# Two-block network on one core: head norms and the GLA gate multiplied on VectorE, with a new table of shifts

## The reference

```python
def rms_norm(x, g):
    y = x * rsqrt(mean(x * x, axis=-1) + EPS)
    return y * g

def gla_output(o, gate, norm_g, w_o):              # o: tokens x 4 heads x 128
    o = rms_norm(o, norm_g).reshape(b_, t_, GLA_V)
    return (o * silu(gate)) @ w_o

def attn_heads(q, k, v, qn_g, kn_g, tabs):         # q: 8 heads of 64, k: 2 heads of 64
    q, k = rms_norm(q, qn_g), rms_norm(k, kn_g)
    if tabs is not None:                           # latent tokens only
        q, k = rope_2d(q, tabs), rope_2d(k, tabs)
    return q, k, v
```

## Time and profile before

| | |
|---|---|
| median of three runs | 1309.15 us (1308.46 to 1309.38) |
| the profiled execution | 1308.85 us |
| its span, first to last instruction | 1306.9 us |
| mean granted clock of TensorE | 0.976 |
| VectorE busy | 896.9 us, 1636 instructions |
| ScalarE busy | 587.8 us, 978 instructions |
| GpSimd busy | 295.4 us, 235 instructions |

### The profile page before, as it was taken

The page is one execution under the profiler, slowest core; times in us unless marked ns, Lnnn a source line. Parts: engine busy times, 40 slices in busy tenths (PEclk is TensorE's granted clock), DMA queues, the critical chain, the costliest instruction groups (busy, mean ns, idle before and its releaser), DMA issues. The chain is left out here.

```text
span 1306.9 us, 19578 instructions
## 1 busy us (share of the span) xinstructions
PE 1226.5 (94%) x7720; PEld 1003.4 (77%) x7720; DVE 896.9 (69%) x1636; ACT 587.8 (45%) x978; POOL 295.4 (23%) x235
## 2 busy tenths in 40 slices
PE   6899997989998999995999999999999989799998
PEld 5767876768877778774777778888898768579997
DVE  4598766786787443798999464435776687866655
ACT  3445542445555544222433444324563554337543
POOL 0210103210115313347000030311451241201223
PEclk9999997989999999998999999999999998989999
DMA  7575476454533411121222212333653233214453
GB/s 247 202 286 189 162 268 208 164 198 146 203 129 116 142 53 61 50 65 64 81 66 65 65 65 81 97 97 105 207 175 104 82 108 97 65 36 144 156 182 113
DMA packets 49132, 168.10 MB, mean 129 GB/s; under 512 B 5841, under 2 KB 7057, under 8 KB 48785
## 3 DMA queue, kind: packets, MB, share of 16 engines
q1 hardware_dynamic: 49041, 166.86, 38.3%
HBM read 165.79 MB, written 1.05 MB: 128 GB/s over the span
## 5 line engine op out<-in xcount | busy, mean ns | idle before, releaser
L2385 DVE TENSOR_TENSOR w_lo<-w_raw,w_hi 128x1024 fp32r<-128x1024 f32 (+3 forms) x264 | 322.1, 1223 | 187.2 <-ACT w_hi L1965 186.0
L1965 ACT ACTIVATE w_hi<-w_raw 128x1024 fp32r<-128x1024 f32 (+3 forms) x264 | 270.1, 1026 | 377.0 <-issue 118.7
L1581 PE MATMUL bank<-w_hi,x_hi 128*128 128x512 f32 (+4 forms) x736 | 297.8, 405 | 16.8 <-DVE w_lo L2385 14.4
L1583 PE MATMUL bank<-w_hi,x_lo 128*128 128x512 f32 (+4 forms) x736 | 280.8, 382 | 0.0
L1582 PE MATMUL bank<-w_lo,x_hi 128*128 128x512 f32 (+4 forms) x736 | 280.4, 381 | 0.0
L1599 PE MATMUL bank<-x_hi,w_hi 128*128 128x512 f32 (+1 forms) x640 | 224.8, 351 | 1.5 <-DVE w_lo L2385 1.5
L1601 PE MATMUL bank<-x_lo,w_hi 128*128 128x512 f32 (+1 forms) x640 | 216.4, 338 | 0.0
L1600 PE MATMUL bank<-x_hi,w_lo 128*128 128x512 f32 (+1 forms) x640 | 216.3, 338 | 0.0
L1581 PEld LDWEIGHTS bank<-w_hi,x_hi 128*128 128x128 f32 x736 | 141.4, 192 | 50.1 <-DVE w_lo L2385 18.2
L1583 PEld LDWEIGHTS bank<-w_hi,x_lo 128*128 128x128 f32 x736 | 140.4, 191 | 26.9
L1582 PEld LDWEIGHTS bank<-w_lo,x_hi 128*128 128x128 f32 x736 | 141.4, 192 | 22.6
(11 more groups left out here) (359 smaller groups left out, 1801.5 us busy)
## 6 DMA issues: line engine op xcount, KB each, us to landing
w_raw<-in_w SPq DMA_DIRECT2D x172, 512.0 KB, 3.6
w_raw<-in_wm SPq DMA_DIRECT2D x48, 512.0 KB, 5.0
w_raw<-in_wo SPq DMA_DIRECT2D x40, 512.0 KB, 4.3
w_raw<-in_wy_gla SPq DMA_DIRECT2D x8, 512.0 KB, 3.5
w_raw<-in_wy_att SPq DMA_DIRECT2D x8, 512.0 KB, 3.5
w_raw<-in_wy_conv SPq DMA_DIRECT2D x8, 512.0 KB, 3.5
w_raw<-in_w SPq DMA_DIRECT2D x8, 460.0 KB, 5.0
w_raw<-in_w SPq DMA_DIRECT2D x12, 288.0 KB, 2.8
```

What stands on the lines that cost most here:

```text
L1581: mm(out, xh[:, q, col], hi[:, kk, 0:w], start=kp == 0 and kk == 0 and not with_bias, stop=False)
L1583: ins = mm(out, xl[:, q, col], hi[:, kk, 0:w], start=False, stop=last and kk == KP - 1)
L1965: do(hi, raw, ACT.Copy).then_inc(sem["cut_hi"], 1)
L2385: v.tensor_tensor(lo, raw, hi.bitcast(F32), ALU.subtract).then_inc(sem["cut_lo"], 1)
```

## The change

In a head norm GpSimd's hr_iv keeps only the power. VectorE's hr_n multiplies each head by its root and by the norm weight in one instruction of 64 columns, 8 for a query tile and 2 for a key tile. In the GLA output gla_n is gone, and gated moves to VectorE: four instructions of 128 columns multiply each head by its root and by the gate. gla_iv on GpSimd keeps its power and its product with the norm weight. The first step of the next layer that overwrites the sums (gla_ms) now waits for gated where it waited for gla_n. The product of attention and gate (y2_gate) stays on GpSimd and has a semaphore of its own. HASTE is replaced and some lengths too, so that the planner orders all engines anew, in the first block as well.

```diff
-            yield [("gla_sq", l, t), ("gla_ms", l, t), ("gla_iv", l, t), ("gla_n", l, t)]
+            yield [("gla_sq", l, t), ("gla_ms", l, t), ("gla_iv", l, t)]
...
-    "att_t_act fox": 0.3, "bias1": -0.4, "conv_ve": 1.5, "flip mix": 3, "gla_ki": -0.4, "gla_m": 6, "ln_dve": 3,
-    "loads_consts": 1.5, "lr_t": 3, "mi_x": 0.3, "mod_col": 0.8, "out_gate": 0.3, "project_y y2": 0.3}
+    "att_t_act fox": 0.3, "bias1": -0.4, "conv_g": -0.4, "conv_n": -1, "conv_silu": -0.4, "conv_ve": 1.5, "ev_ag": -0.4,
+    "ev_gate": -1, "ev_y y0": 0.3, "flip mix": 3, "flip_hi mix": 3, "fox_cols": 1.5, "gla_ki": -0.4, "gla_m": 6, "gla_tot": 6,
+    "heads_act dq": -3, "heads_dve iq": -1, "hr_add q": 1.5, "hr_iv k": 3, "hr_sq q": -0.4, "ln_dve": 3, "ln_stat": 6,
+    "loads_consts": 1.5, "lr_t": 3, "mi_act": 3, "mi_pow": 0.3, "mi_x": -0.4, "out_gate": 0.3, "project_y y2": 0.3,
+    "sub_sum": -0.4, "y2_lo": 6}
...
-    "gate_silu": 0.45, "gated": 1.95, "gla_a": 0.86, "gla_con": 0.6, "gla_cp": 1.85, "gla_cum": 0.85, "gla_dec": 0.2,
+    "gate_silu": 0.45, "gated": 1.0, "gla_a": 0.86, "gla_con": 0.6, "gla_cp": 1.85, "gla_cum": 0.85, "gla_dec": 0.14,
...
-    "gla_one": 0.54, "gla_qf": 0.43, "gla_qi": 0.6, "gla_qt": 0.48, "gla_sq": 1.25, "gla_st": 0.55, "gla_tot": 0.9,
-    "gla_z": 0.85, "gla_zero": 2.2, "heads": 0.43, "heads_act": 0.48, "heads_dve": 0.6, "hr_add": 1.25, "hr_iv": 2.3,
-    "hr_ms": 0.6, "hr_n": 1.4, "hr_sq": 1.25, "index_iw": 0.1, "index_relu": 0.45, "index_sel": 0.2, "index_top": 0.6,
+    "gla_qf": 0.3, "gla_qi": 0.89, "gla_qt": 0.48, "gla_sq": 1.25, "gla_st": 0.55, "gla_tot": 0.9, "gla_z": 1.0,
+    "gla_zero": 2.2, "heads": 0.43, "heads_act": 0.48, "heads_dve": 0.6, "hr_add": 0.96, "hr_iv": 1.58, "hr_ms": 0.6,
+    "hr_n": 1.8, "hr_sq": 1.25, "index_iw": 0.1, "index_relu": 0.45, "index_sel": 0.14, "index_top": 0.6, "index_w": 0.5,
...
-    "gated": lambda l, c, t: [("ev_gate", l, c, t), ("gla_n", l, t)],
+    "gated": lambda l, c, t: [("ev_gate", l, c, t), ("gla_iv", l, t)],
...
-    def gla_n(l, t):
-        ov = b.gv[:, t, :].rearrange("p (h n) -> p h n", h=4)
+    def gated(l, c, t):
+        dve.wait_ge("ev_gate", l, c, t)
         dve.wait_ge("gla_iv", l, t)
-        v.tensor_tensor(ov, ov, b.gms[:, t, 0:4].unsqueeze(2).to_broadcast([P, 4, P]), ALU.mult).then_inc(sem["gla_n"], 1)
+        for h in range(4):
+            part, gate = b.gv[:, t, h * P:(h + 1) * P], k.gate_home(l, t)[:, h * P:(h + 1) * P]
+            ins = v.scalar_tensor_tensor(part, part, b.gms[:, t, h:h + 1], gate, ALU.mult, ALU.mult)
+        ins.then_inc(sem["gated"], 1)
...
-        ins = v.tensor_tensor(view, view, stat[:, 2, 0:n_heads].unsqueeze(2).to_broadcast([P, n_heads, HD]), ALU.mult)
+        dve.wait_ge("consts2_in", CONSTS2)
+        for h in range(n_heads):
+            ins = v.scalar_tensor_tensor(view[:, h, :], view[:, h, :], stat[:, 2, h:h + 1], b.rows[:, l, first:first + HD], ALU.mult, ALU.mult)
...
-    def gated(l, c, t):
-        pool.wait_ge("ev_gate", l, c, t)
-        pool.wait_ge("gla_n", l, t)
-        g.tensor_tensor(b.gv[:, t, :], b.gv[:, t, :], k.gate_home(l, t), ALU.mult).then_inc(sem["gated"], 1)
...
-        g.tensor_tensor(stat[:, 2, 0:n_heads], stat[:, 1, 0:n_heads], m.half[:, 0:n_heads], ALU.pow)
-        pool.wait_ge("consts2_in", CONSTS2)
-        pool.wait_ge("hr_sq", l, what, t)
-        g.tensor_tensor(view, view, spread(gain, [P, n_heads, HD]), ALU.mult).then_inc(sem["hr_iv"], 1)
+        g.tensor_tensor(stat[:, 2, 0:n_heads], stat[:, 1, 0:n_heads], m.half[:, 0:n_heads], ALU.pow).then_inc(sem["hr_iv"], 1)
```

More of the change, by code:

```diff
@@ L759 @@
[L759 to L762, removed]
@@ new lines @@
+    "hr_n": 1.8, "hr_sq": 1.25, "index_iw": 0.1, "index_relu": 0.45, "index_sel": 0.14, "index_top": 0.6, "index_w": 0.5,
+    "lam": 0.4, "lam_dots": 0.74, "lam_exp": 0.2, "ln_dve": 1.3, "ln_pool": 3.24, "ln_pow": 0.32, "ln_stat": 0.17, "ln_x": 0.52,
+    "load": 2.0, "lr_flip": 0.43, "lr_t": 0.48, "m_hi": 0.55, "m_lo": 0.6, "mean_w": 0.2, "mi_act": 0.98, "mi_add": 1.0,
+    "mi_dve": 0.6, "mi_flip": 0.43, "mi_hi": 0.55, "mi_lo": 0.78, "mi_ms": 0.1, "mi_pow": 0.71, "mi_sq": 1.1, "mi_x": 1.04,
@@ L959 @@
     "gla_sq": lambda l, t: [("gla_o1", l, t), ("gla_o2", l, t)],
-    "gla_ms": lambda l, t: [("gla_sq", l, t), ("gla_n", l - 1, t)],
+    "gla_ms": lambda l, t: [("gla_sq", l, t), ("gated", l - 1, GG, t)],
     "gla_iv": lambda l, t: [("gla_ms", l, t)],
-    "gla_n": lambda l, t: [("gla_iv", l, t)],
     "hr_sq": lambda l, what, t: [*BLOCK1_OVER, ("ev2", l, KKV if what == "k" else AQ, t)],
@@ L1032 @@
           "ln_dve": "ln_steps", "conv_ve": "conv_steps", "conv_rs": "conv_steps", "conv_dev": "conv_steps",
-          "conv_n": "conv_steps", "ev_ag": "ev_gate", "y2_gate": "gated", "y2_hi": "flip_hi", "y2_lo": "flip_lo"}
+          "conv_n": "conv_steps", "ev_ag": "ev_gate", "y2_hi": "flip_hi", "y2_lo": "flip_lo"}
 def signal_of(stage):
@@ L2828, in gla_ms @@
         if l > 0:
-            dve.wait_ge("gla_n", l - 1, t)
+            dve.wait_ge("gated", l - 1, GG, t)
         one = dve.own(v.tensor_reduce(b.gms[:, t, 0:4], b.gtmp[:, g, :].rearrange("p (h n) -> p h n", h=4), AXX, ALU.add))
@@ L2854, in hr_n @@
     def hr_n(l, what, t):
-        src, n_heads, stat = head_view(what, t)
+        src, n_heads, stat, first = head_view(what, t)
         view = src.rearrange("p (h d) -> p h d", d=HD)
         dve.wait_ge("hr_iv", l, what, t)
-        ins = v.tensor_tensor(view, view, stat[:, 2, 0:n_heads].unsqueeze(2).to_broadcast([P, n_heads, HD]), ALU.mult)
+        dve.wait_ge("consts2_in", CONSTS2)
+        for h in range(n_heads):
+            ins = v.scalar_tensor_tensor(view[:, h, :], view[:, h, :], stat[:, 2, h:h + 1], b.rows[:, l, first:first + HD], ALU.mult, ALU.mult)
         if t in X_TILES:
@@ L2955, in vector_engine @@
              "gla_one": gla_one, "gla_la": gla_la, "gla_qi": gla_qi, "gla_kt": gla_kt, "gla_m": gla_m, "gla_st": gla_st,
-             "gla_o2": gla_o2, "gla_ms": gla_ms, "gla_n": gla_n, "hr_ms": hr_ms, "hr_n": hr_n, "ak_t": ak_t,
+             "gla_o2": gla_o2, "gla_ms": gla_ms, "gated": gated, "hr_ms": hr_ms, "hr_n": hr_n, "ak_t": ak_t,
              "aq_dve": aq_dve, "a_max": a_max, "a_inv": a_inv, "a_t_dve": a_t_dve, "att_out2": att_out2,
@@ L3109, in gla_iv, with head_view @@
         g.tensor_tensor(ov, ov, spread(b.rows[:, l, 0:P], [P, 4, P]), ALU.mult).then_inc(sem["gla_iv"], 1)
-    def head_view(what, t, l):
+    def head_view(what, t):
         if what == "k":
-            return b.kkv[:, t, QK2:QK2 + P], AKV, b.ams[:, 0, t], b.rows[:, l, P + HD:P + 2 * HD]
-        return b.aq[:, t, :], AH, b.ams[:, 1, t], b.rows[:, l, P:P + HD]
+            return b.kkv[:, t, QK2:QK2 + P], AKV, b.ams[:, 0, t]
+        return b.aq[:, t, :], AH, b.ams[:, 1, t]
     def hr_sq(l, what, t):
-        src, n_heads, stat, gain = head_view(what, t, l)
+        src, n_heads, stat = head_view(what, t)
         i, before = slot("gtmp", "hr_sq", l, what, t)
@@ L3125, in hr_iv @@
     def hr_iv(l, what, t):
-        src, n_heads, stat, gain = head_view(what, t, l)
-        view = src.rearrange("p (h d) -> p h d", d=HD)
+        _, n_heads, stat = head_view(what, t)
         pool.wait_ge("hr_ms", l, what, t)
-        g.tensor_tensor(stat[:, 2, 0:n_heads], stat[:, 1, 0:n_heads], m.half[:, 0:n_heads], ALU.pow)
-        pool.wait_ge("consts2_in", CONSTS2)
-        pool.wait_ge("hr_sq", l, what, t)
-        g.tensor_tensor(view, view, spread(gain, [P, n_heads, HD]), ALU.mult).then_inc(sem["hr_iv"], 1)
+        g.tensor_tensor(stat[:, 2, 0:n_heads], stat[:, 1, 0:n_heads], m.half[:, 0:n_heads], ALU.pow).then_inc(sem["hr_iv"], 1)
     def hr_add(l, what, t):
-        src, n_heads, stat, gain = head_view(what, t, l)
+        src, n_heads, stat = head_view(what, t)
         i, j = slot("gtmp", "hr_sq", l, what, t)[0], slot("gtmp", "hr_n", l, what, t)[0]
```

33 lines of the change are left out of this document (17 added, 16 removed).

## The result

| | before | after |
|---|---|---|
| median of 4 runs each, same chip | 1308.81 us (1308.32 to 1309.38) | 1287.46 us (1285.43 to 1288.97) |
| ratio, 95% interval | | 0.9842 (0.983 to 0.9855) |
| profiled execution, its span | 1308.85, 1306.9 | 1286.08, 1284.8 |
| TensorE busy, and waiting inside the span | 1226.5, 80.4 | 1218.5, 66.3 |

A forecast was written before the change was run, and what follows sets the result against it. TensorE, busy 1226.5 of 1306.9 us, was taken as the bound, so only its waits and half clock count. From 1308.85 us, 9.5 (first place), 4 (second) and 0 (table) gave 1295.35, median 1295.7 us, range 1281 to 1314.

The forecast's parts named there:

- Prices of the new instructions: VectorE's small products, priced from conv taps: 1.6 us per query tile, 0.46 per key tile, 1.12 per gated tile.
- VectorE's net: VectorE's added minus removed products: 9.5 us more, up to 12 back from less GpSimd slowing; none put on the path.
- The first place: TensorE's wait near 598 us for layer 0's GLA gated product, with half clock behind: gain 9.5 us, bounds 6 and 12.5.
- rival (a): Head-norm chain or VectorE's in-order queue still delays gating; wait moves only a few us: gain 2 to 5, about 1305; chance 0.15.
- The second place: Wait of layer 1's query transposes for tile 1's norm, with half clock to 1088.0: gain 4 us, bounds 1.7 and 9.5.
- The table: New shifts and lengths reorder every engine in both blocks; sign unknown, taken as 0 with -8 to +8 us.
- The sum: Profiled execution 1308.85 - 9.5 - 4 + 0 = 1295.35 us; median of the runs 0.3 above it, 1295.7 us.
- The tests that the prediction named: No TensorE wait over 3 us before gla_v or att_q transposes, clock near 1.0 around 600 and 1075; also signs of being wrong.
- One sign of being wrong: Anywhere in the kernel: half clock in a stretch that has full clock in the kernel before.
- (c): VectorE becomes the bound from 570 to 625 us, its added products ahead of weights' low parts: 1317 us; chance 0.07.
- (d): New table opens a wait like the first elsewhere, 10 us with its slow clock: 1309 to 1318 us; chance 0.15.
- (e): Change doesn't do what it says: 9.5 us of GLA weight products stay on GpSimd; no chance of its own.

The follow-up runs named there:

- the unneeded ones: Kernel after plus one 512-column product nobody reads on GpSimd behind each of the four powers of layer 0's query norms, written order unchanged: 1291.16 us.
- products alone: Kernel after with the shifts and lengths of the kernel before, except the lengths of the steps that the moved products touch: 1292.28 us.
- tables alone: Kernel before with the new shifts and lengths, except the lengths of the four steps that the products touch; products stay on GpSimd: 1300.67 us.
- tap shift in layer 0 alone: Kernel after with a planner shift of -1 for the conv taps of layer 0 in the second block, layer 1 at 0: 1282.91 us.
- truer lengths: Kernel after with the planner given the lengths its trace shows for the head norms' root, weight and rotation, and for the power: 1309.39 us.
- gate alone: Kernel after, but with head norms' weight products on GpSimd and root product whole, with their lengths, as before: 1296.93 us.
- heads alone: Kernel after, but with the GLA norm's root product and the gated product on GpSimd as before: 1298.93 us.

## Why the prediction was right, and where only by luck of the sum

**Prices of the new instructions: right.** Eight products of 64 columns were put at 1.6 us and take 1.65 where GpSimd stands still; four of 128 at 1.12 and take 1.14. The groups of the kernel after:

```profile
L2865 DVE SCALAR_TENSOR_TENSOR att_q<-att_q,att_ms,rows 128x64 f32<-128x64 f32 x48 | 11.7, 316 | 1.6 <-POOL att_ms L3129 1.6
...
L2841 DVE SCALAR_TENSOR_TENSOR gla_v<-gla_v,gla_ms,merged 128x128 f32<-128x128 f32 x24 | 7.0, 354 | 0.0
...
L2865 DVE SCALAR_TENSOR_TENSOR gla_k_att_kv<-gla_k_att_kv,att_ms,rows 128x64 f32<-128x64 f32 x16 | 4.0, 288 | 1.6 <-POOL att_ms L3129 1.6
```

The mean of one is longer than its share of the sum (316 ns against 11.7/48 = 244), since neighbours overlap; whoever multiplies the mean by the count pays too much. The Trainium skill (VectorE: DVE Perf Modes, errata of SBUF sources) states its formula for an fp32 add of 512 and of 2048 columns; carried down to these sizes, as an estimate, eight of them would be 1.79 us and four of 128 1.16. The trace is 8% and 2% below that.

**VectorE's net: right in the sum.** It was put at 9.5 us more, with up to 12 back from GpSimd's silence. The sum of VectorE is +0.8 us: 22.7 added, 7.1 + 2.3 and 4.5 (the root product of the GLA norm) removed, so 8.0 of other work got shorter. That products on GpSimd can cost VectorE as much is shown by the unneeded ones. But not all of the 8.0 is the relief that the prediction meant: with products alone VectorE's sum is 901.4 us, +4.5, so 3.7 come with the table. The low parts of x_mod, for one, far from the moved products, took 15.3 us before and 14.4 with products alone, and take 11.6 with tables alone and 11.5 in the kernel after.

**The first place: the mechanism of rival (a), the size between it and the forecast.** The step that failed is the sentence that TensorE finds tile 0 gated "unless VectorE's own queue holds it". It does: the product that could start at 584.3 starts at 594.92. I had the condition and took it as the exception. The forecast was 9.5 us with a lower bound of 6; the stage gave 5.5. Two kernels with the same work in another written order show that the order is the cause: with the tap shift in layer 0 alone the gated product starts 3.7 us earlier, and 6.2 us are gained by the 161st low part; with the truer lengths, which write it ahead of the root product of tile 2, the wait for it is 3.8 us. Taps are only a part of what stands ahead of it; the steps of the query norm are the larger. The wait for the query norms, which the sum put at 0 to 4 us, did not come. Half clock behind the wait stayed as it was (5.4 us of work before, 5.2 after), where the sum had allowed at most 2.

**The second place: right in size, by luck in part.** 4 us were forecast, nearer the lower bound; 0.9 of wait and 2.3 of clock are 3.2. The kernel with unneeded products has the same written order and half clock for 10.24 us there, so the part of the clock is not firm.

**Layer 1's tail: not forecast.** Of the 8.5 us of the last stage 5.3 remain. TensorE's waits outside the second place are 3.5 us less there (15.2 to 11.7), most of them short ones in layer 1's attention, and half clock there is 10.24 us from 1120.14, before 13.65 from 1142.44. Of the whole last stage products alone give 8.1 us, tables and gate alone nothing, and heads alone 2.4, which is no more than timing alone moves. So it takes both kinds of product, in the runs at hand. Whether the cause is an order of VectorE that neither makes alone, and which step in it counts, stays open.

**The table: wrong in the sum, inside its bounds.** It stood at 0 with -8 to +8. By itself it is worth 7.6 us by the medians; in its trace 7.1 lie in the first block and 3.5 at the first place, less 1.9 behind them. In the first block of the kernel after TensorE waits 4.1 us less than before (41.9 to 37.8), in no single large piece (of the two waits for x, 4.3 us, which the prediction had named, one of 1.9 stays, and one of 3.1 for a low part stands in place of the other), and is busy 4.1 us less for the same matmuls. Of that second half 3.0 us show with products alone too, in the written order of before; they are no effect of the table, and what they are stays open.

**The sum.** Forecast 9.5 + 4 + 0 = 13.5. In the trace 5.5 (first place), 3.2 (second), 5.3 (layer 1's tail), 8.2 (first block), -0.1 between: 22.1. Right in direction and range, but 4 us too much at the first place stood against 13.5 us that the sum had at nothing.

**The tests that the prediction named.** Of those for right two failed, though a gain of 21 us came all the same: no wait over 3 us (7.4 and 4.6 stayed), and a clock near 1.0 around 600 (half until 601.3). GpSimd 271.6 against 270, VectorE 897.7 against 900, waits for weights 12.2 against a limit of 25 were as said. The transposes of att_q wait 4.6, just under the 5 that would have refuted it. One sign of being wrong did show, in small: 3.41 us of half clock from 14.23, where before has full clock. The sum did not change by it: the first block has 23.9 us at half in both traces. Rivals (c) and (d) are out: TensorE waits less for low parts of weights, and no wait like the first opened elsewhere; the largest new one is 3.1 us, for a low part in the first block. Of (e) it is true that GLA's weight products stay on GpSimd (six, 8.9 us); no long wait of TensorE is for them.

## What to carry to other kernels

Work that leaves a queue is worth what stands behind it in that queue, minus what now stands before it in the next one: when a step is moved to another engine whose order is written out, look up its neighbours there before its duration. A table of shifts that feeds such an order is no small term: with the same work, single entries moved this kernel by 22, 75 and 81 us (the last from 1282.91 to 1363.76), so run it alone, and give a shift to the stage that needs it rather than to all. And sum the stages between the same points of the work, not only the named waits; here 13.5 of 22 us lay outside the two places. A difference of 2 or 3 us in one stage of two single traces needs no cause: kernels with the same written order differed by as much here.

## What the runs showed of the hardware that was not expected

- A product of 1.35 us on GpSimd lengthens VectorE's small products beside it by 1.0 us (1.65 to 2.67 and 2.69; beside a square as well, 2.42 to 3.45). The Trainium skill (GPSIMD Engine Reference, Key points) says that GpSimd contends with VectorE instructions that have two SBUF inputs, and the traces agree.
- Half clock is not in proportion to the wait at which it begins. At the first place 9.85 us of wait stand with 10.24 us at half, 7.41 with 10.24, 8.10 (gate alone) with 6.83, 4.79 (layer 0's tap shift) with 6.83; at the second 5.5 with 10.24, 4.58 with 3.41, 3.10 (products alone) with 10.24, and 3.98 with 1.90 (unneeded products) with 10.24. It can begin inside the wait, so what it costs is half of the part in which TensorE works. The prediction made it shrink with the wait; the runs don't bear that out, and most of the second place's gain (2.3 of 3.2 us) hangs on it.
- Many small waits can cost more clock than one long one. With the query transposes late, 39 us of idle time in pieces of at most 2.3 us stand in 130 us at a mean granted clock of 0.63, that is 96 us at half; the single wait of 19.9 us (taps 1 us later) had 27.3 us at half by it.
- One VectorE instruction of 64 columns behind another of its kind costs 1.65/8 = 0.21 us, so eight small ones with two factors (1.65) cost about one us more than a single one of 512 columns with one factor (0.69) and replace a second pass of 2.0 us on another engine.
